# Recurrent mixer of a two-block model: 64-column moving operands, with GpSimd building the block-diagonal stationary copies

## The reference, cut to what matters

```python
def step(s, inp):
    w, kk, a, k, v, r = inp
    sa = jnp.einsum('dbhij,dbhj->dbhi', s, kk)
    s = s * w[..., None, :] - sa[..., :, None] * (kk * a)[..., None, :] + v[..., :, None] * k[..., None, :]
    return s, jnp.einsum('dbhij,dbhj->dbhi', s, r)
return lax.scan(step, s0, scan_in)          # 256 context tokens, then 512 tokens
```

## Time and profile before

| | µs |
|---|---|
| median of 3 runs | 4775.67 |
| lowest, highest | 4772.65, 4778.11 |
| span of the profiled execution | 4773.1 |
| the stretch in which mixer units are built, about | 2093 to 3109 |
| two units, from slot 0 of one to slot 0 of the next but one | 130.2 |

### The profile page before, as it was taken

How to read it: one execution, slowest core, us unless ns; L and a number is a source line. 1 busy time by engine, 2 the same in 40 slices (tenths; PEclk the granted TensorE clock), 3 DMA queues, 4 the chain that set the end, 5 groups by cost and what they waited for, 6 DMA issues and landing times. The chain is left out here.

```text
span 4773.1 us, 57369 instructions
## 1 busy us (share of the span) xinstructions
PE 4295.2 (90%) x20622; PEld 3153.4 (66%) x20622; DVE 3084.4 (65%) x6230; ACT 1654.8 (35%) x3360; POOL 850.6 (18%) x866
## 2 busy tenths in 40 slices
PE   8989999989998999989999999989899887777777
PEld 6657887747887877879888888968644333333332
DVE  5664434674434767567777777634577888888885
ACT  3354233353242356135555455432211111111111
POOL 1101010101011012000000000000134444444443
PEclk9999999999998999989999999989999988999989
DMA  4213433213433102310000000033599999999998
GB/s 131 67 40 128 146 124 98 82 40 106 148 126 117 62 18 97 103 36 12 15 11 7 15 15 15 1 132 111 197 388 416 421 413 413 413 411 415 409 415 345
DMA packets 150587, 794.50 MB, mean 166 GB/s; under 512 B 19880, under 2 KB 23192, under 8 KB 83488
## 3 DMA queue, kind: packets, MB, share of 16 engines
q0 software_dynamic: 84544, 575.18, 29.9%
q1 hardware_dynamic: 58272, 188.32, 12.0%
q10 hardware_dynamic: 7488, 27.30, 1.8%
HBM read 766.53 MB, written 20.00 MB: 165 GB/s over the span
## 5 line engine op out<-in xcount | busy, mean ns | idle before, releaser
L3255 PE MATMUL psum<-rows,diag 128*128 128x512 f32 x2048 | 1003.6, 640 | 228.1 <-ACT diag L3134 209.4
L3255 PEld LDWEIGHTS psum<-rows,diag 128*128 128x128 f32 x2048 | 408.3, 204 | 779.8 <-issue 766.8
L2996 DVE SCALAR_TENSOR_TENSOR uh<-rows,h_rows 128x1024 f32<-128x1024 f32 x512 | 628.3, 1227 | 205.1 <-DMA rows<-in_peer_uv,sel_idx 178.6
L2953 POOL DMA_INDIRECT rows<-in_peer_uv,sel_idx x512 | 611.2, 1194 | 739.0 <-PE psum L3255 677.4
L529 DVE TENSOR_TENSOR w_split_lo<-w_raw,w_split_hi 128x1024 fp32r<-128x1024 f32 (+1 forms) x271 | 325.0, 1209 | 498.8 <-ACT w_split_hi L516 494.7
L516 ACT CAST w_split_hi<-w_raw 128x1024 fp32r<-128x1024 f32 (+1 forms) x271 | 276.5, 1028 | 616.2 <-PE psum L465 397.3
L3127 ACT ACTIVATE g<-g 128x4 f32<-128x4 f32 x128 | 26.3, 205 | 1090.2 <-DVE g L3007 1090.2
L2079 PE MATMUL psum<-x,wAT_wide 128*128 128x128 f32 x1920 | 254.5, 276 | 1.4 <-DVE x L2444 1.0
L2079 PEld LDWEIGHTS psum<-x,wAT_wide 128*128 128x128 f32 x1920 | 237.4, 192 | 18.4 <-issue 15.0
L693 POOL TENSOR_TENSOR uT_lo<-normed_rows,uT_hi 128x512 fp32r<-128x512 f32 x64 | 90.2, 1409 | 664.8 <-ACT uT_hi L669 664.8
L465 PE MATMUL psum<-hT_mlp_hi,w_split_hi 128*128 128x512 f32 x512 | 201.1, 393 | 4.7 <-DVE hT_mlp_lo L261 4.6
(11 more groups left out here) (538 smaller groups left out, 9356.7 us busy)
## 6 DMA issues: line engine op xcount, KB each, us to landing
w_raw<-in_w_in SPq DMA_DIRECT2D x105, 512.0 KB, 4.3
w_raw<-in_w_up SPq DMA_DIRECT2D x64, 512.0 KB, 4.2
w_raw<-in_w_down SPq DMA_DIRECT2D x64, 512.0 KB, 4.2
amask_sb<-in_w_mod ACTq DMA_DIRECT2D x48, 512.0 KB, 4.5
wq<-in_peer_wq SPq DMA_DIRECT2D x24, 512.0 KB, 7.7
rows<-in_peer_uv,sel_idx POOLq DMA_INDIRECT x512, 12.6
qkpad<-in_w_out SPq DMA_DIRECT2D x12, 512.0 KB, 5.1
w_raw<-in_w_out SPq DMA_DIRECT2D x12, 512.0 KB, 3.9
```

The lines of the kernel that those rows point to most:

```text
L2953: nc.gpsimd.indirect_dma_start(out=rows[:, n % RB, :], out_offset=None, in_=I["peer_uv"], in_offset=bass.IndirectOffsetOnAxis(ap=sel[:, t, ...
L2996: nc.vector.scalar_tensor_tensor(prod[:], rows[:, n % RB, 0:D], 1.0, h[:, t, :], ALU.mult, ALU.mult, accum_out=dots[:, (n // BATCH) % 2, s ...
L3255: last = nc.tensor.matmul(psum[:, 2 * (t % 2) + half, :], diag[:, n % (2 * BATCH), :], rows[:, n % RB, D + half * NB:D + (half + 1) * NB], ...
```

## The change

It changes which operand of the mixer's products moves and which engine does the copies around them.

- `X`, `U`, a new `Yn`, the values `vC`, the state `wS`, `wN` and `wW` are stored with 64 columns for a chunk, head 0's above head 1's. Where they are moving operands, 64 columns stream instead of 128. Stationary operands stay block-diagonal with 128 columns: `wAT`, `Y`, `wBT`, `wbt`, `wkt`, `wq`.
- VectorE writes and transposes 256 columns for four chunks instead of 512, and ScalarE's copy to `U` has 256.
- GpSimd gets a program: it presets `Yn` with the identity, copies `Yn` into the diagonal blocks of `Y` after each level (`widen_y`, two copies of 64 partitions by 256), copies `wS` and `wN` of the output chunks into `Sw` and `Nw` (`widen_s`, `widen_n`, two copies of 64 by 64), and the values into `wV` (`widen_v`).
- At the last level `Y` is no longer completed by a predicated copy: its product has `Y` stationary, as at the other levels, and VectorE transposes two blocks of it from PSUM straight into `Y`.
- The decayed old state is added by a product with the identity (`ident`·`wS`) in PSUM, and ScalarE, not VectorE, writes the new `wS`, scaled by `pl`. `wP` goes. `wS` and `wN` have two buffers.
- Outputs are formed transposed, channels by tokens, with `wV`, `Sw` and `Nw` stationary and 64 columns of `Cc`, `qr`, `Dd` moving; both directions add up in one PSUM bank, and one copy by ScalarE (slot 4) takes it. The output of chunk n is issued one step later, behind `N` of chunk n + 1. `y_rows`, its two VectorE steps and the transposes of rows go.
- On TensorE and ScalarE `scan(k)` now stands ahead of `solve(k)`.

```diff
-                        last = nc.tensor.matmul(psum[:, b, i * P:(i + 1) * P], flat(wAT[:, c]), flat(X[:, c]),
+                        last = nc.tensor.matmul(psum[:, b, i * L_CH:(i + 1) * L_CH], flat(wAT[:, c]), X[:, c],
...
-                    if lv > 1:
-                        pe.wait_ge(y_back, 12 * u + 3 * (lv - 2) + b + 1)
+                    pe.wait_ge(y_wide, 2 * n)
...
+                    if n > CCH:
+                        output(n - 1, u)
+                elif n < NCH - 1:
...
+                    nc.tensor.matmul(S_, flat(wkt[:, u % 2, c]), v, start=True, stop=False)
+                    if n:
+                        nc.tensor.matmul(S_, ident[:], wS[:, n % 2], start=False, stop=False)
                     pe.wait_ge(n_copied, 12 * u + n + 1)
...
+                nc.tensor.matmul(y, flat(wV[:, g % 2, c]), Cc[:, u % 2, x_], start=opens, stop=False)
+                pe.wait_ge(s_wide, 16 * u + 2 * (n - CCH + 1))
+                nc.tensor.matmul(y, flat(Sw[:, n % 2]), qr[:, r_slot(u), c * L_CH:(c + 1) * L_CH], start=False, stop=False)
+                pe.wait_ge(n_wide, 16 * u + 2 * (n - CCH + 1))
+                nc.tensor.matmul(y, flat(Nw[:, n % 2]), Dd[:, u % 2, x_], start=False, stop=closes).then_inc(y_done, 1)
...
+            def widen_y(lv, b, u):
+                if lv == 0:
+                    pool.wait_ge(y_opened, 3 * u + b + 1)
...
+                else:
+                    pool.wait_ge(y_back, 12 * u + 3 * (lv - 1) + b + 1)
+                for h, at in halves():
+                    nc.gpsimd.tensor_copy(Y[at, u % 2, batch(b), h, :], Yn[at, batch(b), :]).then_inc(y_wide, 1)
...
+            def widen_n(n, u):
+                pool.wait_ge(n_copied, 12 * u + n + 1)
+                if u or n >= 6:
+                    pool.wait_ge(y_done, 8 * u + n - 5)
+                for h, at in halves():
+                    nc.gpsimd.tensor_copy(Nw[at, n % 2, h, :], wN[at, n % 2, :]).then_inc(n_wide, 1)
...
+                    nc.scalar.activation(wS[:, (n + 1) % 2], psum[:, 5, 0:L_CH], ACT.Copy, scale=pl[:, u % 3, c:c + 1]
+                                         ).then_inc(s_copied, 1)
...
-                    nc.vector.scalar_tensor_tensor(wS[:], psum[:, 5, 0:P], scale, wP[:], ALU.mult, ALU.add
-                                                   ).then_inc(s_copied, 1)
...
+                    for h in range(2):
+                        to, fr = 64 * h + 32 * d, 64 * h + 32 * (1 - d)
+                        last = nc.vector.transpose(
```

More of the change, by code:

```diff
@@ L1941, in r_slot, with solved, halves @@
         return 1 + u % 3
-    def two(ap, u, c):
-        return ap[:, u % 2, c:c + 2].rearrange("p c t -> p (c t)")
-    def slot_of(ap, u):
-        return ap[:, u % 2]
+    def solved(b):
+        return psum[:, b, 0:4 * L_CH]
+    def halves():
+        return [(h, slice(64 * h, 64 * h + 64)) for h in range(2)]
     def norm_bank(g, half):
@@ new lines, in widen_v @@
+            def widen_v(g):
+                pool.wait_ge(v_copied, 7 * (g + 1))
+                if g >= 2:
+                    pool.wait_ge(y_done, 16 * (g - 1))
+                for h, at in halves():
+                    nc.gpsimd.tensor_copy(wV[at, g % 2, :, h, :], vC[at, g % 2]).then_inc(v_wide, 1)
+            for wide in (Y, Sw, Nw):
+                nc.gpsimd.memset(wide[:], 0.0).then_inc(sides_zero, 1)
+            pool.wait_ge(sides_zero, 3)
+            for b in range(3):
+                preset(b)
@@ new lines, in _ @@
+            for i in ITERATIONS:
+                build, scanned, prep, norm, tile, final = stages(i)
+                for k in range(SLOTS_):
+                    n, step = divmod(k, 3)
+                    if scanned is not None and n >= CCH:
+                        if step == 0:
+                            widen_s(n, scanned)
+                        elif step == 2:
+                            widen_n(n, scanned)
+                    if build is not None:
+                        if k < 3:
+                            widen_y(0, k, build)
+                        else:
+                            lv, half, b = solve_step(k)
+                            if lv < LEVELS and half == 1:
+                                widen_y(lv, b, build)
+                    if tile is not None and k == V_WIDE_AT:
+                        widen_v(tile)
@@ L2132, in scan @@
                         pe.wait_ge(s_copied, 11 * u + n)
-                        last = nc.tensor.matmul(W, flat(wq[:, u % 2, c]), wS[:], start=False, stop=True)
+                        last = nc.tensor.matmul(W, flat(wq[:, u % 2, c]), wS[:, n % 2], start=False, stop=True)
                     last.then_inc(w_ready, 1)
@@ L2249, in _ @@
                 for k in range(SLOTS_):
+                    if scanned is not None:
+                        scan(k, scanned)
+                    if k == 0 and 0 <= i - 2 < UNITS:
+                        output(NCH - 1, i - 2)
                     if build is not None:
@@ L2253, in _ @@
                             fill(k, build)
-                    if scanned is not None:
-                        scan(k, scanned)
                     if prep and k in (0, 2, 4, 6):
@@ L2393, in _ @@
                         exps(k, prep)
-                    if prep is not None and k in PRESET_AT:
-                        preset(PRESET_AT[k], prep)
                     if tile is not None and k in TURNED_AT:
@@ L2603, in _ @@
                         solve(k, build)
-                    if scanned is not None and k % 3 == 2 and k < SLOTS_ - 1:
-                        state(k // 3, scanned)
                     if build is not None:
@@ L2609, in _ @@
                             fill(k, build)
-                    if scanned is not None and k in (24, 35):
-                        outputs(k // 35, scanned)
                     if tile is not None and k in (6, 11):
@@ L2719, in rwkv_constants @@
     out["incl"] = np.stack(incl, 1).astype(f)
-    lev = np.zeros((P, 2, LEVELS + 1, L_CH), f)
-    for i in range(LEVELS + 1):
+    lev = np.zeros((P, 2, LEVELS, L_CH), f)
+    for i in range(LEVELS):
         m = 2 ** i
@@ L2725, in rwkv_constants @@
         lev[:, 1, i] = 1.0 * (same & ((row // m) % 2 == 0) & ((col // m) % 2 == 1))
-    out["level"] = np.tile(lev, (1, 1, 1, 2)) * out["ones"][:, None, None, :]
+    out["level"] = lev
+    out["eye"] = (row == col).astype(f)
     tt = np.arange(N_ALL)
```

226 lines of the change are left out of this document (109 added, 117 removed).

## The result

The changed kernel takes 5003.2 µs (median of four runs, 4990.4 to 5045.7), the kernel before in the same session 4774.2. The ratio is 1.049, 95% interval 1.045 to 1.054: slower by 4.9%, where 4773 was forecast, with 4742 to 4815 as the range. The profiled execution is the slowest of the four, 5045.7.

The account below looks back on a forecast made before the run. TensorE was taken to bound the mixer, busy 121.9 of 130.2 µs in two units. Pairs -22, first unit -2, clock +13 and last scan +8 gave -3, so 4773 µs, range 4742 to 4815.

Parts of the forecast that it names:

- Passes at 0.112: TensorE's narrow passes: halved columns hardly shorten one, about 0.112 each, only the first of a run 0.056 shorter.
- The identity's +4.5: New product with the identity on TensorE: 10 chunks a unit, two passes, 40 x 0.112 = +4.5 for two units.
- Waits of ScalarE: TensorE waiting for ScalarE's scan copies: 1.0 a unit at slot 9, 1.4 at slot 19 (odd), twice 0.5 at slots 33, 34.
- rival 3: GpSimd's queue is late, copies at twice the price beside VectorE's two-operand steps: +35, 4808; chance 0.15.
- +13: Clock term of the sum: eight falls at slot 19 of odd iterations, 1.6 lost at each.
- The 1.6: Loss per clock fall, from one dip before: 3.3 µs at 1.2 GHz, 16 passes instead of some 30.
- the 0.7 for GpSimd: TensorE's wait for `Nw` behind GpSimd's in-order widenings in the output: 0.7 a unit, 1.4 for two, lower bound 0.
- Rival 2: Clock falls often among narrow passes, slots 18 to 33, 1.6 each: 4797 (one more a unit) to 4845 (three); chance 0.15.
- The last scan: Last unit's scan: output products between `N` and state, more at low clock, less `y_rows`, transposes and a copy: +8.
- The sum without the clock: Two units: passes +3.2 and waits -6.1, so -2.9 against 130.2.
- rival 1: Clock holds and GpSimd hides: -32, about 4744, or 4754 with GpSimd's wait; chance 0.30.
- The prediction's -24: Gain before clock and last scan: -22 for 7.5 pairs with a scan beside the build, -2 for the first unit.

Follow-up runs that it names:

- Experiment two: Kernel before, with only both solve products streaming 64 columns instead of 128: 4780.4 µs, ratio 1.0007.
- experiment six: Kernel of experiment five, with V widened in slot 33 instead of 28: 4796.7 µs (1.0042 to 1.0069).
- experiment seven: Kernel of experiment six, with GpSimd's presets of `Yn` moved behind the last level's widening, to slots 30 to 32: 4744.0 µs, 0.9935.
- Experiments five: Kernel of experiment three, with ScalarE's square root in slot 18 behind the copy of W: 4788.6 µs, 1.0039.
- experiment three: Changed kernel, with the third output product (`Nw`) one slot later and V widened in slot 28 instead of 19: 4806.1 µs, 1.0089.
- experiments four: Changed kernel, with solve products streaming 128 columns, third output product a slot later and V widened in slot 28: 4760.6 µs, 0.9971.

## Why the prediction was wrong, point by point

**Passes at 0.112: right.** Eight narrow passes take 0.89 to 0.90 among narrow ones, and the 0.056 saved at the head of a run is there: behind wider passes at full clock the second narrow pass starts 0.056 to 0.058 behind the first, not 0.112. Experiment two shows 0.3 a unit from width and no more. The identity's +4.5 was 3.4 in effect.

**Waits of ScalarE: right.** ("By spacing" means from start to start, less the 0.112 of a pass.) Slot 9: 1.0 forecast, 0.91 recorded and 1.07 by spacing, in every paired unit. Slot 19, odd: 1.4 forecast, 1.23 recorded and 1.39 by spacing. Slots 33 and 34: twice 0.5 forecast; one of 0.46 (0.61 at half clock), in slot 34.

**GpSimd: right place, wrong size.** The prediction had it "with VectorE 0.8 late from reciprocals (odd) or with the 1.7 of `widen_v` in front of chunk 6 (even) I get 0.7 a unit". By spacing it is 1.7 (odd, chunk 8) and 2.9 (even, chunk 6), 3.2 more for two units, 24 in all. The terms that were mis-sized are durations beside VectorE. Even: V took 2.3 instead of 1.7, and the two copies to `Nw` 1.9 instead of 0.6; 0.7 + 0.6 + 1.3 = 2.6. Odd: two copies of 64x256 took 1.64 and a preset 1.20 instead of 0.9 each (the rows of experiment six); 0.7 + 0.7 + 0.3 = 1.7. That leaves 0.3 of the even wait unexplained. I had spread the collision evenly over all copies (rival 3, factor two), but it is uneven and strongest where TensorE waits: over the two units a 64x64 copy took 0.25 or 0.30 on average, and 0.84 and 1.01 here. Each of the two ended 0.1 behind the end of a two-operand VectorE step, 2580.92 and 2581.98. Rival 3's 35 was about the size of this part; it was not the part that counted.

**The clock: the step that failed.** The sum has +13, eight falls at slot 19 of odd iterations with 1.6 lost at each, and +8 for the last scan. No run shows the 13: the clock measured some +302 in the profiled execution and +227 to +269 in the others, last scan included. Nor does halving the columns lower the grant by itself: experiment seven, with every pass of solve, scan and outputs narrow, kept 1.00 for 780 µs. The place was right: falls do start at slot 19 in odd units. Two things were not.
- *How long a fall lasts.* The 1.6 came from a single dip in before, where wide passes followed at once. I took its length as a property of the fall. It is one of what follows: behind the wait of slot 19 the gate product with 512 columns is near, and the stay was 3.4 to 6.8 in four of six units; behind the waits for `Nw` nothing wide comes for long, and it was 24 in most odd and 44 to 48 in most even units. Half of that is the loss: 12 to 24, not 1.6. Twice the gate product missed, and the fall of slot 19 lasted 51.
- *Which waits start one.* I had the 0.7 for GpSimd as harmless in the likeliest case. At 1.7 and 2.9 they started most of the long stays (nine of thirteen; a tenth followed one of 0.85 in the second unit). Experiments five and six show that 0.79 can be enough: a stay followed eleven of twelve such waits there, but none of six in the profiled execution of experiment three. What decides between them stays open.

Rival 2 had this mechanism and even the point from which it decides ("a wait of 0.7 among narrow passes"), with 0.15. Its price, 1.6 a fall, was the same wrong number, so that its worst case was 4845. The argument against it, "nearly every place of TensorE's queue is filled there", is refuted by the row with 39.0 of 39.3 busy at 0.50: full places didn't bring the clock back among narrow passes.

**The last scan.** +8 forecast; from 32.3 at a mean grant of 0.95 to 48.1 at 0.50, so +16.

**The first unit**, built alone: -2 forecast; 50.6 to 49.0 in experiment three, where its clock held. In the changed kernel its own fall made it 58.4.

**The sum without the clock: right.** 127.3 for two units forecast with GpSimd's 1.4. Experiment three, all narrow and with 0.79 for GpSimd, has 129.7, less half of one stay of 6.8: 126.3, or 126.9 with 1.4. With the clock held by removing waits, experiment seven gives 4744, the very number of rival 1. That match is luck in part: rival 1 kept the 1.4 of slot 19, which seven lacks, and had only +2 for the last scan, which stays at half clock in seven. The prediction's -24 was real and is what the last kernels build on.

## What to carry to other kernels

Before halving the moving columns of passes whose weight loads stand as far apart as the passes themselves (0.1125 and 0.112 here), note that it saved 0.3 a unit in experiment two and left a stream that, once the clock had fallen, was busy for 39.0 of 39.3 µs and didn't bring it back. Either keep the width (a moving operand read twice through a step of 0 cost 0.3 a unit here, and the stays of paired units were 3.4 to 6.8 µs instead of 24 and more), or make sure that no wait like the 0.79 ahead of eleven stays here is left in the narrow stretch. Price a fall of the clock by the distance to the next wide work behind it (all 21 stays ended 1.9 to 5.2 behind the start of such), not by the dip seen elsewhere (3.3 here, where 24 to 51 came). When a helper engine with one queue feeds a chain, look at what stands in that queue when it runs late (the presets of `Yn` here, two copies of 64x256 in 1.20), not at its place in the program.

## What the runs showed of the hardware

- **The same stream stood at either clock.** Fully placed passes of 64 columns held a grant of 1.00 for 780 µs (764 busy, experiment seven), and at 0.50 such a stream, busy 39.0 of 39.3 µs, did not raise it (changed kernel). The falls with a long stay behind them whose start is told above stood behind waits of 0.79 to 2.9.
- **The shortest wait ahead of a long stay.** Among narrow passes one of 0.79 µs preceded each of the eleven stays of 17 to 24 in experiments five and six, while seven such waits there and in experiment three had none behind them. With 128 columns in the solve products 2.76 went by at 1.00, in other units 3.4 to 6.8 µs at half clock followed.
- **What stood ahead of a return.** Every one of the 21 in the changed kernel's mixer came 1.9 to 5.2 µs behind the start of passes of 128 to 512 columns; two passes of 512 at 2275.5 had one behind them and two at another place had not. What decides between them stays open.
- **Reading a moving operand twice** costs next to nothing. Eight passes take 0.95 instead of 0.89, but the narrow pair behind them takes 0.17 instead of 0.23, so the ten take 1.12 either way (2505.31 to 2506.43, 2577.70 to 2578.82). Over a whole even unit it is 62.7 against 62.4 (experiments four and three).
- **A 64x64 copy of GpSimd** takes 0.23 to 0.24 alone; two beside two-operand steps of VectorE took 0.84 and 1.01.
